# The first norm's gain vector: spread over the rows, or turned into columns

## The reference, cut to what matters

```
def _rms_norm(x, g):
    y = x * rsqrt(mean(x * x, axis=-1) + 1e-6)      # one factor per token (row)
    return y * g                                    # one factor per channel (column)

h = _rms_norm(x, norm_mix_pre)        # (512, 1024)
z = h @ w_in_first                    # q, k, v | r, k, v | decay, rate and gate inputs
...                                   # attention, a recurrent scan, output product, FFN, second block
```

## Time and profile before

| | |
|---|---|
| time, median of 3 runs | 1240.69 us (1240.66 to 1241.28) |
| time of the profiled execution | 1239.91 us |
| its span, first to last instruction | 1238.2 us |
| mean granted clock of PE | 0.997 |
| PE / DVE / ACT / POOL busy | 97% / 70% / 54% / 34% |
| first matmul of the `G_LORA` tile starts at | 16.18 us |
| third tile of the next product starts at | 41.75 us |

### The profile page before, as it was taken

The page is one execution under the profiler, slowest core; times in us unless marked ns, Lnnn a source line. Parts: engine busy times, 40 slices in busy tenths (PEclk is TensorE's granted clock), DMA queues, the critical chain, the costliest instruction groups (busy, mean ns, idle before and its releaser), DMA issues.

```text
span 1238.2 us, 26863 instructions
## 1 busy us (share of the span) xinstructions
PE 1205.6 (97%) x11189; PEld 1103.8 (89%) x11189; DVE 871.9 (70%) x1153; ACT 664.1 (54%) x1154; POOL 420.7 (34%) x345
## 2 busy tenths in 40 slices
PE   8999999998999999999999999999999999999998
PEld 6777797787898999999999997866889999999997
DVE  6678646566468689887895666435576897888953
ACT  4555536557355447456475544544454474564652
POOL 7022226333005247267261141000052472672500
PEclk9999999999999999999999999999999999999999
DMA  6223300002343233333344232122232333333331
GB/s 203 69 68 102 102 2 2 4 3 81 131 150 121 69 103 104 102 103 113 92 171 154 77 107 82 35 69 86 69 101 70 103 103 103 103 107 99 103 120 69
DMA packets 103231, 113.10 MB, mean 91 GB/s; under 512 B 2099, under 2 KB 97381, under 8 KB 103110
## 3 DMA queue, kind: packets, MB, share of 16 engines
q1 hardware_dynamic: 103030, 111.12, 28.4%
q0 software_dynamic: 80, 0.26, 0.1%
HBM read 107.18 MB, written 4.19 MB: 90 GB/s over the span
## 4 chain that ended last, share of the span: by engine, by line
PE 84%; DVE 7%; ACT 4%; issue 2%; DVEq 1%; ACTq 1%; POOL 1%; POOLq 0%
PE ps L627 8%; PE ps L628 7%; PE ps L629 7%; PE ps L718 5%; PE ps L719 5%; PE ps L720 5%; PE ps L591 4%; PE ps L593 4%; PE ps L592 4%; PE ps L773 3%; PE ps L775 3%; PE ps L774 3%; PE ps L678 1%; PE ps L680 1%; PE ps L679 1%
## 5 line engine op out<-in xcount | busy, mean ns | idle before, releaser
L627 PE MATMUL ps<-w_hi,a_hi 128*128 128x256 f32 x640 | 179.5, 280 | 0.3
L628 PE MATMUL ps<-w_lo,a_hi 128*128 128x256 f32 x640 | 178.8, 279 | 0.0
L629 PE MATMUL ps<-w_hi,a_lo 128*128 128x256 f32 x640 | 178.5, 279 | 0.0
L2065 DVE TENSOR_TENSOR w_lo<-w_raw,w_hi 128x2048 fp32r<-128x2048 f32 (+1 forms) x43 | 98.1, 2282 | 45.5 <-ACT w_hi L1398 45.2
L627 PEld LDWEIGHTS ps<-w_hi,a_hi 128*128 128x128 f32 x640 | 120.2, 188 | 1.2 <-DVE w_lo L2194 1.1
L628 PEld LDWEIGHTS ps<-w_lo,a_hi 128*128 128x128 f32 x640 | 120.3, 188 | 0.1
L629 PEld LDWEIGHTS ps<-w_hi,a_lo 128*128 128x128 f32 x640 | 120.3, 188 | 0.0
L718 PE MATMUL ps<-th,w_hi 128*128 128x256 f32 x384 | 109.2, 284 | 1.6 <-ACT tmp L1496 1.6
L720 PE MATMUL ps<-th,w_lo 128*128 128x256 f32 x384 | 107.9, 281 | 0.0
L719 PE MATMUL ps<-tl,w_hi 128*128 128x256 f32 x384 | 107.8, 281 | 0.0
L2173 DVE TENSOR_TENSOR w_lo<-w_raw,w_hi 128x1024 fp32r<-128x1024 f32 (+1 forms) x72 | 100.0, 1403 | 4.4 <-ACT w_hi L1471 4.4
(11 more groups left out here) (467 smaller groups left out, 3885.2 us busy)
## 6 DMA issues: line engine op xcount, KB each, us to landing
w_raw<-w_ffn_up_dram SPq DMA_DIRECT2D x16, 1024.0 KB, 5.7
w_raw<-w_ffn_down_dram SPq DMA_DIRECT2D x16, 1024.0 KB, 5.3
w_raw<-w_up_dram SPq DMA_DIRECT2D x16, 1024.0 KB, 5.8
w_raw<-w_down_dram SPq DMA_DIRECT2D x16, 1024.0 KB, 5.2
w_raw<-w_in_first_dram SPq DMA_DIRECT2D x12, 1024.0 KB, 5.4
w_raw<-w_out_dram SPq DMA_DIRECT2D x8, 1024.0 KB, 5.2
xn<-x_dram SPq DMA_DIRECT2D x8, 512.0 KB, 6.0
w_raw<-w_in_dram SPq DMA_DIRECT2D x4, 1024.0 KB, 6.3
```

The costliest lines, as they stand in the source:

```text
L627: mm(o, hi[:, hb + k, tok], whi, start=first and own and k == ks[0], stop=False, skip_group_check=True)
L628: mm(o, hi[:, hb + k, tok], wlo, start=False, stop=False, skip_group_check=True)
L629: m = mm(o, lo[:, hb + k, tok], whi, start=False, stop=last and k == ks[-1], skip_group_check=True)
L2065: v.tensor_tensor(w_lo[:, g % 2, :, 0:n], w_raw[:, g % 2, :, 0:n], w_hi[:, g % 2, :, 0:n].bitcast(F32), ALU.subtract).then_inc(sm["w_lo_re ...
```

## The change

The gain is no longer spread over the rows. It lands as 8 rows of 128 values, and one small transpose of 8x128 on PE turns them into 8 columns, which ACT copies to a new tile `gain` of 128x8. DVE's pass over the rows multiplies by the inverse root alone. The gain comes in where the turned rows are copied: there channels are on the partitions, so a slice's gain is one value for each partition. That makes one instruction of 128x128 for each slice, with its own column of `gain`: four where there was one, in `first_upper` on ACT and in `first_lower` on DVE. DVE's wait for the gain moves from ahead of the rows to ahead of the lower parts.

```diff
+        gain = sb("gain", [P, KT])
...
-            sp.dma_start(gpre[0:1, :], a["norm_mix_pre"][0:1, :]).then_inc(sm["row_loaded"], 16)
+            sp.dma_start(gpre[0:KT, 0:P], a["norm_mix_pre"][0].rearrange("(k p) -> k p", p=P)).then_inc(sm["row_loaded"], 16)
...
                     pe.wait_ge(sm["row_loaded"], 16)
-                    for b in range(2):
-                        m = mm(ps[:, 2 + b, :], ones[0:1, :], gpre[0:1, b * S:(b + 1) * S], start=True, stop=True)
-                    m.then_inc(sm["gain_spread"], 1)
+                    nc.tensor.transpose(ps[:, 2, 0:KT], gpre[0:KT, 0:P], ident[0:KT, 0:KT]).then_inc(sm["gain_turned"], 1)
...
+            def first_upper(c):
+
+                for b in range(2):
+                    act.wait_ge(sm["rows_turned"], 2 * c + b + 1)
+                    for k in range(4 * b, 4 * b + 4):
+                        m = af(h_hi[:, k, rows(c)], by_k(ps[:, 4 + 2 * (c % 2) + b, :])[:, k % 4, :], ACT.Copy, scale=gain[:, k:k + 1])
+                    m.then_inc(sm["hhi_ready"], 1)
...
             first_root(0)
+            act.wait_ge(sm["gain_turned"], 1)
+            af(gain[:, :], ps[:, 2, 0:KT], ACT.Copy).then_inc(sm["gain_ready"], 1)
             first_root(1)
             split(G_LORA, n=160)
-            upper(N_MIX1, 0)
-            upper(N_MIX1, 1)
+            first_upper(0)
+            first_upper(1)
...
-                scaled_rows(c, c, hn[c % 2], ps[:, 2:4, :].rearrange("q a s -> q (a s)")).then_inc(sm["hn_ready"], 1)
-
-            dve.wait_ge(sm["gain_spread"], 1)
+                v.tensor_scalar(hn[c % 2], xn[:, c, :], sd[:, c:c + 1], None, ALU.mult).then_inc(sm["hn_ready"], 1)
+
+            def first_lower(c):
+
+                for b in range(2):
+                    dve.wait_ge(sm["hhi_ready"], H_MIX1 + 2 * c + b + 1)
+                    for k in range(4 * b, 4 * b + 4):
+                        m = v.scalar_tensor_tensor(out=h_lo[:, k, rows(c)], in0=by_k(ps[:, 4 + 2 * (c % 2) + b, :])[:, k % 4, :],
+                                                   scalar=gain[:, k:k + 1], in1=h_hi[:, k, rows(c)].bitcast(F32),
+                                                   op0=ALU.mult, op1=ALU.subtract)
+                    m.then_inc(sm["hlo_ready"], 1)
+
             first_rows(0)
             first_rows(1)
             split(G_LORA, n=160)
-            lower_rows(N_MIX1, 0)
-            lower_rows(N_MIX1, 1)
+            dve.wait_ge(sm["gain_ready"], 1)
+            first_lower(0)
+            first_lower(1)
```

More of the change, by code:

```diff
@@ L258, in program @@
         names = (
-            "consts_built", "eps_built", "row_loaded", "gain_spread", "page_loaded", "page_turned", "par_ready", "lora_loaded", "wpool_loaded",
+            "consts_built", "eps_built", "row_loaded", "gain_turned", "gain_ready", "page_loaded", "page_turned", "par_ready", "lora_loaded", "wpool_loaded",
             "gain_loaded", "part_squared", "pre_ready", "sd_ready", "x_rows_ready", "hn_ready", "rows_turned", "slot_free",
@@ L1665, in _ @@
             first_root(0)
+            act.wait_ge(sm["gain_turned"], 1)
+            af(gain[:, :], ps[:, 2, 0:KT], ACT.Copy).then_inc(sm["gain_ready"], 1)
             first_root(1)
             split(G_LORA, n=160)
-            upper(N_MIX1, 0)
-            upper(N_MIX1, 1)
+            first_upper(0)
+            first_upper(1)
             first_root(2)
             first_root(3)
-            upper(N_MIX1, 2)
-            upper(N_MIX1, 3)
+            first_upper(2)
+            first_upper(3)
             split(G_RKV)
@@ L2416, in _ @@
             split(G_LORA, n=160)
-            lower_rows(N_MIX1, 0)
-            lower_rows(N_MIX1, 1)
+            dve.wait_ge(sm["gain_ready"], 1)
+            first_lower(0)
+            first_lower(1)
             first_rows(2)
             first_rows(3)
-            lower_rows(N_MIX1, 2)
-            lower_rows(N_MIX1, 3)
+            first_lower(2)
+            first_lower(3)
             split(G_RKV)
```

## The result

| | before | after |
|---|---|---|
| time, median | 1240.69 us (1239.88 to 1242.76, 5 runs) | 1247.93 us (1246.63 to 1249.41, 5 runs) |
| ratio, 95% interval | | 1.0058 [1.0047, 1.0069] |
| profiled execution, its span | 1239.91, 1238.2 us | 1246.63, 1244.8 us |

The change makes the kernel 7.2 us slower, well outside the range that was given. The opening went nearly as worked out. Most of the loss came from the rest of the program, of which the change touches no line.

A forecast was written before the change was run, and what follows sets the result against it. PE, 97% busy, was taken as the bound, its opening held by spreading the gain. Terms -1.9 + 2.1 = +0.2 us, plus 1.1 for the clock, gave +1.3 on 1240.69: 1242.0 us, range 1240.0 to 1243.6.

The forecast's parts named there:

- Rows in one input: DVE's pass over rows in the opening, multiplying by the root alone: 0.75 us for 1024 elements against 1.28.
- pieces: Copies of 128x128 for each slice in the opening: 0.25 us apart on ACT, 0.27 on DVE.
- PE's first tile: PE's first real work in the opening was to start at 14.4, 1.8 us earlier.
- a fall of the clock behind PE's pause: A pause of 2.4 to 3.8 us before 14.4 lowers PE's clock: 1.1 us on the path, bounds 0 and 2.7.
- ACT's split of `G_RKV`: ACT's split of the second weight group: ends at 23.8 instead of 23.6, or later by the clock's cost.
- a wait of 2.03 us for DVE ahead of the third tile: PE's wait in the next product: 1.4 us instead of 0.19, the tile starting between 41.9 and 43.
- The opening without a fall: Opening's sum with the clock held, -1.9 + 2.1 = +0.2 us, 1240.9; chance 0.34 together with Rival E.
- Rival E: Opening: the gain row lands late in eight parts, so the change removes nothing; share of a joint chance of 0.34.
- A: The forecast: clock falls in the opening's longer pause, partly on the path; +0.2 + 1.1 = +1.3 us; chance 0.47.
- rival C: Clock fall covers PE's whole first tile: +0.2 + 2.7 = +2.9 us, 1243.6; chance 0.14 with others of that size.
- all that changes lies there: The premise that the change acts only within the first 42 us, so only those timelines were followed.
- covers in the queues of POOL and SP: POOL, SP's queue and DMA costed at nothing: order kept; DVE first needs POOL's work at 25.9, POOL's being at 7.6.

The follow-up runs named there:

- e5: e2's kernel with 28 more transposes of the identity in PE's pause; 1243.07 us, ratio 1.0020.
- e16: The changed kernel with 64 unused bytes behind `gain`; 1236.42 us, ratio 0.9972.
- e2: The changed kernel with `gain` as a view of 8 columns of an existing tile, so no tile moves; 1242.90 us, ratio 1.0022.
- e4: The kernel before with an unused tile of 32 bytes ahead of all tiles, so weights move with the rest; 1240.73 us, ratio 1.0008.
- e20: The opening of e6 at the places of e15 (96 unused bytes); 1236.62 us, ratio 0.9971.
- e9: The changed kernel with 96 unused bytes behind `gain`, so later tiles move by 128 bytes; 1247.47 us, ratio 1.0056.
- e15: The kernel before with 96 unused bytes behind `eps`; 1233.88 us, ratio 0.9956.
- e19: The kernel before with 192 unused bytes behind `eps`; 1250.25 us, ratio 1.0080.
- e13: The kernel before with 256 unused bytes behind `eps`; 1240.54 us, ratio 1.0000.
- e14: The kernel before with 512 unused bytes behind `eps`; 1239.60 us, ratio 0.9993.
- e6: No tile moved: chunks 0 and 1 the changed way, 2 and 3 the old, gain spread in PE's pause with 20 more transposes; 1241.97 us, ratio 1.0008.

## Why the prediction was wrong

**What held.** Rows in one input of 0.75 us (later ones; the first two took 1.14 and 0.92); pieces 0.26 us apart (0.25 and 0.27 said); PE's first tile at 14.14 (14.4); a fall of the clock behind PE's pause; ACT's split of `G_RKV` ending at 25.25 (23.8, or later by what the clock took); a wait of 2.03 us for DVE ahead of the third tile, at 43.29, a little later than said. The opening without a fall was said to cost +0.2 us and came to 0.16 in e5. Rival E had nothing to it: the small transpose ran at 6.06, where the spreading had started at 6.07. That the clock fell in this execution was in part luck, since it did not in e16.

**A term mis-sized.** A gave the opening +1.3 us, 1.1 of it the clock, since "part of such a fall lies in the pause itself". None of it did: the pause ended at 14.14, and the matmuls were 0.21 us apart only from 14.82 on. The fall's price was the whole of what the prediction had worked out for one, 1.5 us, and e5 against e2 measured 1.57. That is rival C's mechanism more than A's. That the longer pause would bring a fall at all was my estimate from the falls in the earlier trace rows, and the runs have it both ways: behind 3.79 us idle the clock fell in the changed kernel, behind 3.58 in e16 it did not. e2 as a whole cost +2.7 us [ratio 1.0022, 1.0013 to 1.0031], and C had said +2.9. e2's trace has +1.6 us of it at 44 us and 2.1 at the end; the profiled execution was among the fastest of e2's, and the rest of the median's 2.7 is not placed.

**A slip that moved nothing.** From the prediction's own terms PE's wait ahead of the third tile is 0.19 + 1.2 + 0.2 = 1.6 us, not 1.4.

**The step that failed** is "all that changes lies there", the opening. The diff's first line, a tile of 32 bytes, was given no cost, and none of the rivals spoke of it. What the runs showed in its place: it moved every later operand to another distance from the weights, and some 7,500 matmuls changed their spacing (e1: +6.2 us from an unused tile alone; e4: no change if the weights move along). The prediction looked for covers in the queues of POOL and SP, and did not look at the layout of the memory.

**Open.** Why the distance modulo 256 bytes matters, and why the wide and the narrow forms answer to it differently, no run shows; nor why executions at 64 differ. Nor is it settled which waits make the clock fall: behind waits of PE of 2.03 us at 43.29 in the changed kernel and 1.97 at 41.23 in e20 it did not, behind 2.07 at 42.17 in e5, 2.48 at 42.30 in e16 and 1.80 at 43.14 in e9 it did. One opening had both outcomes.

## What to carry to other kernels

Here an unused tile of 32 bytes a partition cost 6.2 us through what is allocated behind it (e1), and the same values in bytes that were there already left the spacings at 117.6 and 233.1 ns (e2). So read the layout as part of the diff, put such a tile last or into free bytes, and compare the spacing of matmuls far from the edit first. Where PE is the bound (97% busy here), try a few pads between weights and activations; the eight distances tried here spanned 16 us (1233.88 in e15 to 1250.25 in e19). Follow a gain at one wait of PE past the next ones: e5 won 1.57 us over e2 at DVE's split, and behind its wait of 2.07 us at 42.17 the granted clock was 0.50 (43.50 to 46.80).

## What the runs showed of the hardware

- The spacing of matmuls in this three-pass float32 scheme depends on the distance of their two operands in SBUF (119.9 and 228.1 ns in e1, with that distance changed by 32 bytes, 117.5 and 233.1 in e4, with all moved alike), and steps of 256 and 512 bytes change it by no more than 0.1 ns (e13, e14). Over the distances tried the means were 115.4 to 119.9 ns for the narrow ones and 228.1 to 234.0 for the wide. In the changed kernel the narrow ones near the end were regular, 24 in 2.88 us. The fastest and the slowest of the eight distances are 16.4 us apart (e15, e19).
- Transposes alone came to the closer spacing. In the changed kernel only transposes stand ahead, one of them 8x8; the ten from 6.26 take 1.95 us to the start of the next group, 0.21 apart until 7.81, and the eight from 8.21 are 0.11 apart. The granted clock reads 1.00 over 6.20 to 7.90 and over 7.95 to 9.30 alike, so the step stands in the distances alone. That 28 transposes in the pause held the clock at 1.00 in e5 is not shown, since e16 held it at 1.00 without them.
- Where the clock falls in the stretch from 300 to 330 us went with up to 2.2 us, from one profiled execution each: against before (fall at 306.1) e13 and e14, which have none, gain 1.1 and 1.0 us between 305 and 405 us, and e6, which has it at 320.8, loses 1.1. It differs between executions of one kernel too: of 21 executions of the kernel before, taken beside e1 to e4, the three with a mean granted clock of 1.000 took 1239.2, 1239.2 and 1239.8 us, and the median of all was 1240.2.
